# A kernel of two transformer blocks on one Trainium2 core: the values of two groups of attention heads stand together behind every second unit of projection

## The reference, cut to what matters

```python
for qs in range(0, s, Q_BLOCK):                      # forgetting attention, two blocks of 128 queries
    qe = qs + Q_BLOCK
    logits = (jnp.einsum('bhqd,bhkd->bhqk', q[:, :, qs:qe], k[:, :, :qe])
              + cum[:, :, qs:qe, None] - cum[:, :, None, :qe])
    p = jax.nn.softmax(jnp.where(causal, logits, -jnp.inf), axis=-1)
    outs.append(jnp.einsum('bhqk,bhkd->bhqd', p, v[:, :, :qe]))
...
m = jnp.max(scores, axis=-1, keepdims=True)          # window attention
p = jnp.exp(scores - m)
s = jnp.sum(p, axis=-1, keepdims=True)
out = jnp.einsum('bdnqhk,bdnkhe->bdnqhe', p, vc) / s.transpose(0, 1, 2, 4, 3, 5)
```

## Time and profile before

| | |
|---|---|
| median of three runs | 705.66 us (705.50 to 706.17) |
| the profiled execution | 705.47 us, of it 703.7 us in the span |
| PE, matmuls | 687.7 us busy, 98% |
| PE, weight loads (beside the matmuls) | 558.5 us, 79% |
| DVE | 496.7 us, 71% |
| ACT | 381.0 us, 54% |
| DMA | 138.75 MB, mean 197 GB/s |
| chain that ended last, by engine | PE 83%, DVE 7%, ACT 4%, issue 2%, SPq 2%, DMA 2% |

### The profile page before, as it was taken

The page is one execution under the profiler, slowest core; times in us unless marked ns, Lnnn a source line. Parts: engine busy times, 40 slices in busy tenths (PEclk is TensorE's granted clock), DMA queues, the critical chain, the costliest instruction groups (busy, mean ns, idle before and its releaser), DMA issues.

```text
span 703.7 us, 10828 instructions
## 1 busy us (share of the span) xinstructions
PE 687.7 (98%) x4267; PEld 558.5 (79%) x4267; DVE 496.7 (71%) x726; ACT 381.0 (54%) x559; POOL 16.4 (2%) x34
## 2 busy tenths in 40 slices
PE   8899999999999999999999999999999999999996
PEld 4679997777878887877778877778888888888885
DVE  4888988787976779765577889766666555555445
ACT  5457434565655665654565765745474445444344
POOL 6000000000000000000000000000000000000000
PEclk9999999999999999999999999999999999999999
DMA  9999865666896276832444554432656655655511
GB/s 295 367 381 365 287 224 174 204 218 236 302 329 210 57 240 217 280 115 93 145 149 150 183 178 121 150 120 91 196 179 195 207 176 175 190 184 197 187 60 60
DMA packets 74401, 138.75 MB, mean 197 GB/s; under 512 B 5732, under 2 KB 18400, under 8 KB 74352
## 3 DMA queue, kind: packets, MB, share of 16 engines
q1 hardware_dynamic: 72816, 134.92, 58.3%
q10 hardware_dynamic: 736, 1.81, 0.7%
q0 software_dynamic: 800, 1.35, 0.6%
HBM read 137.01 MB, written 1.05 MB: 196 GB/s over the span
## 4 chain that ended last, share of the span: by engine, by line
PE 83%; DVE 7%; ACT 4%; issue 2%; SPq 2%; DMA 2%; DVEq 0%; ACTq 0%
PE G L392 23%; PE G L394 22%; PE G L393 22%; PE T L433 4%; DVE wlo L1108 2%; DMA raw<-in_ret_w_in_dram 2%; PE T L804 1%; PE G L412 1%; PE T L792 1%; PE G L414 1%; PE G L413 1%; DVE arena L1117 1%; SPq L2489 1%; ACT whi L1892 1%; DVE acc L1117 1%
## 5 line engine op out<-in xcount | busy, mean ns | idle before, releaser
L1108 DVE TENSOR_TENSOR wlo<-raw,whi 128x1024 fp32r<-128x1024 f32 x202 | 246.1, 1222 | 119.5 <-ACT whi L1892 119.0
L1892 ACT ACTIVATE whi<-raw 128x1024 fp32r<-128x1024 f32 x202 | 212.6, 1061 | 136.4 <-PE G L394 91.3
L392 PE MATMUL G<-whi,ahi 128*128 128x512 f32 x696 | 281.4, 404 | 0.7 <-DVE wlo L1108 0.7
L394 PE MATMUL G<-whi,alo 128*128 128x512 f32 x696 | 271.8, 390 | 0.0
L393 PE MATMUL G<-wlo,ahi 128*128 128x512 f32 x696 | 271.2, 390 | 0.0
L392 PEld LDWEIGHTS G<-whi,ahi 128*128 128x128 f32 x696 | 130.7, 188 | 30.1 <-DVE wlo L1108 3.0
L394 PEld LDWEIGHTS G<-whi,alo 128*128 128x128 f32 x696 | 130.6, 188 | 28.5
L393 PEld LDWEIGHTS G<-wlo,ahi 128*128 128x128 f32 x696 | 130.9, 188 | 25.5 <-issue 1.0
L1894 ACT ACTIVATE arena<-T,st 128x128 f32<-128x128 f32 (+2 forms) x56 | 21.7, 478 | 33.3 <-DVE st L1502 33.3
L412 PE MATMUL G<-ahi,whi 128*128 128x256 f32 x128 | 36.4, 285 | 0.9 <-DVE wlo L1108 0.9
L1892 ACT ACTIVATE ahi<-T 128x512 fp32r<-128x512 f32 x25 | 15.0, 599 | 40.6 <-PE T L433 40.6
(11 more groups left out here) (245 smaller groups left out, 623.8 us busy)
## 6 DMA issues: line engine op xcount, KB each, us to landing
raw<-in_ret_w_in_dram SPq DMA_DIRECT2D x48, 512.0 KB, 5.4
raw<-in_w_gate_up_dram SPq DMA_DIRECT2D x40, 512.0 KB, 3.6
raw<-in_mod_w_dram SPq DMA_DIRECT2D x32, 512.0 KB, 4.9
raw<-in_fox_w_in_dram SPq DMA_DIRECT2D x32, 512.0 KB, 4.8
raw<-in_w_in_dram SPq DMA_DIRECT2D x28, 512.0 KB, 3.6
raw<-in_w_down_dram SPq DMA_DIRECT2D x22, 512.0 KB, 3.2
arena<-in_mod_w_dram SPq DMA_DIRECT2D x16, 512.0 KB, 10.4
raw<-in_ret_w_out_dram SPq DMA_DIRECT2D x16, 512.0 KB, 5.5
```

The costliest lines, as they stand in the source:

```text
L392: e.matmul(o, ah, wh, start=first and k == 0, stop=False)
L394: done = e.matmul(o, al, wh, start=False, stop=last and k == 1)
L1108: e.tensor_tensor(o, a, b, op).then_inc(sig[name], 1)
L1892: d = e.activation(o, a, f, scale=scale)
```

## The change

`attention_steps` puts the values of groups i - 3 and i - 2 into every second step, i odd, where each step had those of one group. `values` takes bank 0 for an odd group, and bank 3 for an even one.

```diff
 def attention_steps(n):
 
-    return [[("flip", i - 1)] * (1 <= i <= n) + [("logits", i + z) for z in range(2)] * (i < n and i % 2 == 0) + [("values", i - 2)] * (i >= 2)
-            for i in range(n + 2)]
+    return [[("flip", i - 1)] * (1 <= i <= n) + [("logits", i + z) for z in range(2)] * (i < n and i % 2 == 0)
+            + [("values", i - 3 + z) for z in range(2)] * (i >= 3 and i % 2 == 1) for i in range(n + 2)]
...
-                t = bank((name, "values", g), sig[f"{name}_out"], 2 * g + 2, 3)
+                t = bank((name, "values", g), sig[f"{name}_out"], 2 * g + 2, 0 if g % 2 else 3)
```

## The result

The changed kernel took 709.2 us (median of five runs, 707.6 to 709.7), the kernel before 705.7 us (705.5 to 706.67). The ratio is 1.0046, with a 95% interval from 1.0035 to 1.0057: slower by 0.46%. The profiled execution of the changed kernel took 709.7 us, 707.2 of it in the span, 3.5 us more than before.

What follows compares the result with a forecast made beforehand. PE, busy 98% of the span, was taken to bound the kernel. Plain terms of +2.46 us and +1.54 for the clock, on the profiled 705.47, gave 709.5; the median stands 0.19 above, so 709.7 us, range 707.3 to 710.8.

Steps and rivals of the forecast that it cites:

- steps 2 to 8, three pairs: Forgetting attention, groups 0 to 5: each pair of value blocks saves 0.11 us on PE, together -0.33 us.
- step 10, wait for group 7: Forgetting attention: PE's first mask waits for the second `weighted` of DVE, let go at 345.68 instead of 344.93, +0.75 us.
- step 11, unit to `left_of`: Forgetting attention: `left_of` needs group 9's `weighted` and stalls PE 2.84 us; 2.2 or 3.9 also possible.
- the clock: Behind the step 11 stall PE's granted clock falls to 0.50, costing +1.54 us; chance 0.50 as part of the forecast.
- steps 12 and 13: Forgetting attention's end: values 10 move to stand ahead of values 11, saving 0.23 us.
- window attention: Two pairs give -0.22 us and steps 6 and 7 -0.23, together -0.45 us, with no new wait.
- A pair against two blocks: On PE a values block costs 0.61 us before other work, 0.50 before another block: 0.11 us saved per pair.
- Step 6 and the other even steps: Forgetting attention: the mask's new wait for the odd group's `weighted` is over before the mask is due; nothing waits.
- The copy at step 9: DVE's copy of flip 8, ending at 344.31, hangs on ACT and DVE, so it stays where it was.
- the stall alone: Rival: all waits as forecast, but the granted clock stays at its higher level, 708.1 us; chance 0.28.
- Not slower: Rival: DVE comes through step 11 in time, `left_of` never waits; 704.7 us, or 703.7; chance 0.10.
- The waits breed more: Rival: stall of 3.9 us, or late transposes hold up ACT and next units; 710.8 us or more; chance 0.12.

Runs made afterwards that it cites:

- the bank alone: Kernel before with its steps as they were, only the odd groups' values in bank 0 instead of 3: 709.4 us, and 709.61 us once more.
- the repeat: The changed kernel once more, unaltered, beside the kernel before: 708.21 us, ratio 1.004.
- the stall filled: Changed kernel with 24 unused transposes on PE between values 9 and `left_of` at step 11: 707.5 us, ratio 1.0022.

## Why the prediction was right, point by point

Distances on PE in the profiled executions, before and after:

| stretch | forecast | measured | from |
|---|---|---|---|
| steps 2 to 8, three pairs | -0.33 | -0.34 | flip to logits of step 8: 305.96 to 335.63, and 306.02 to 335.35 |
| step 10, wait for group 7 | +0.75 | +0.74 | 1.21 for 0.47 |
| step 10, values 8 gone | -0.61 | -0.60 | mask to unit: 1.57 for 2.17 |
| step 11, unit to `left_of` | +3.33 | +3.48 | 7.53 for 4.05 |
| the clock | +1.54 | +1.46 | 4.71 for 3.25, `left_of` to flip |
| steps 12 and 13 | -0.23 | -0.48 | flip to unit: 2.04 for 2.52 |
| window attention | -0.45 | -0.62 | 29.60 for 30.22 |
| sum | +4.00 | +3.64 | span: +3.5 |

- **What bounds the kernel.** That PE has next to no slack behind the attention held. The distances add up to 3.64 us and the span grew by 3.5. Step 0 was 0.06 us later from the start, and 0.20 us came back between the attentions, at one set of transposes above all: before, they started at 362.77, 0.51 us behind the matmul ahead of them, right after DVE's product into `acc` (361.43 + 1.29 = 362.72); in the changed kernel they follow after 0.23 us. The list of waits doesn't show that wait.
- **A pair against two blocks.** Right to a few hundredths: the second block costs 1.09 - 0.61 = 0.48 us, 0.50 had been reckoned. The rule on a drain at a change of tiling mode (the Trainium skill, TensorEngine Tiling (Array Packing), Key Properties) would have allowed a larger gain. What the traces show is that logits to unit takes as long as logits to values (346.96 - 345.39 = 1.57 us from mask to unit now, 346.49 - 344.93 = 1.56 from mask to values in the earlier trace rows), so leaving out the values there saved the block and no transition on top.
- **Step 6 and the other even steps.** Right: no wait for group 3, 1 or 5, nor in the window attention.
- **The copy at step 9.** The prediction says that it hangs on ACT and DVE and not on PE, "so it is where it was". Had that held, PE would have waited for it until the same moment, and the -0.33 us of the first three pairs would have been lost there, though the sum counts them. The trace shows that the copy moved with PE: it starts at 343.35 instead of 343.63, by 0.28 us, and so do ACT's exponentials of step 8 (337.19 for 337.47) and PE's logits from which they come (335.35 for 335.63). So the sum was right here against its own reasoning.
- **Step 10.** Right in size. The reads of a pair are further apart on DVE than I had taken: the second reciprocal starts 0.11 us after the multiplication before it ended (344.16 + 0.42 to 344.69), where 0.04 had been taken over from reciprocal to multiplication. The wait made up for it by a shorter latency.
- **Step 11.** Right in mechanism, and 0.15 us too small: the same 0.07 us, twice on the way (the pair at step 9, the pair at step 11). That DVE would not catch up the 0.7 us was right: from the copy of flip 8 to the first reciprocal of step 11 it is 9.91 us now (343.35 to 353.26), and 9.17 before (343.63 to 352.80), 0.74 more.
- **Steps 12 and 13.** The sign was right, the size half of what came. The missing term is a wait that the change takes away. In the kernel before, the values of groups 10 and 11 both stand in bank 3 with only `left_of` between them, so those of group 11 had to wait until DVE had read group 10:

```profile
355.87 0.29 DVE L1108 TENSOR_TENSOR acc<-T,st 128x128 f32<-128x128 f32 x1
...
356.30 0.69 PE L804 MATMUL T<-arena 128*64 128x65 f32 x16
```

  The read ends at 355.87 + 0.29 = 356.16 and the values start 0.14 us later, the usual distance from DVE to PE here. The copy of the flip, for which they wait too, had ended at 355.72. From `left_of` to values 11 it took 0.76 us (355.54 to 356.30); in both traces of the bank alone, where group 11 has bank 0, the same sequence takes 0.59 us (359.86 to 360.45 and 359.34 to 359.93), and in the changed kernel, where `left_of` stands behind transposes instead of values, 0.53 (359.63 to 360.16). The difference, 0.76 - 0.53 = 0.23 us, is what the forecast lacked, within 0.02. In the window attention a unit stands between the last two groups, and there each of the first two pairs gave 0.15 us instead of 0.11 (460.32 to 466.96 before, 464.45 to 470.94 after) and the last steps 0.31 instead of 0.23; what these 0.04 to 0.08 us are isn't resolved.
- **The clock.** The price was right: 1.54 us forecast, 1.46 measured, and 1.58 and 1.54 in the two traces of the bank alone (4.83 and 4.79 for 3.25). That it falls was given 0.50 against 0.28 for the stall alone, and both happened, in different executions of one kernel: seven runs to four. The forecast of 709.7 us was that of an execution with the fall, the rival of 708.1 that of one without it (707.3 to 707.7). The median of 709.2 lies near the first because four of these five runs had the fall, which is in part luck: in the repeat it was three of six, and the median 708.21. That the profiled execution took just 709.7 us is luck too, for its span grew by 3.5 us and not by 4.0, and 2.5 us lay around it instead of 1.8. The Trainium skill, TensorE: Matmul & The Clock Gate, Part 1, says that an idle TensorE goes down to 1.2 GHz and that the point at which the clock changes varies from run to run. The traces agree with both: behind stalls of 3.0, 2.2 and 2.2 us the lower level began at 354.20, 354.05 and 354.79 us, before the end of the stall, 0.2 us and 1.4 us after it.
- **The other rivals.** "Not slower" fell with the 2.96 us of waiting. "The waits breed more" fell too: PE's list of waits has no new row for the time behind the stall, neither in the trace with the slow stretch nor in the one without.

## What to carry to other kernels

When work moves to another buffer, list who takes that buffer next and look in the trace for when its reader finishes: the buffer's next user inherits the wait, and here that user was a step that had nothing to do with the values. Where a wait is for a slow engine, look at what that engine does first at that place and whether it is idle just before; reading the values ahead of a weight tile that had not arrived cost nothing and took away the wait of 0.6 us at step 10. And where TensorE bounds the kernel, count a stall on it as more than its length: one of 2 to 3 us cost 1.5 us again in most executions, 13 of 21 by their spans.

## What the runs showed of the hardware

- The same program at the same stall lost the clock in one profiled execution (3.4 us at 0.50) and kept it in another, so one trace doesn't settle whether a stall costs its length or half as much again. Times of the changed kernel spread over 2.1 us and more, those with the stall filled over 0.5.
- The lower clock near 21 us, from which the price was taken, comes and goes as well: of the two traces of the bank alone, the same program, the first has it (23.0 to 26.4 us) and the second does not. There it costs the whole nothing that can be seen. Of the twelve traces seven have it, and the first mask of step 0 starts at 297.04 to 297.59 us in them, and at 297.09 to 297.51 us in the five without it. So a fall has a price behind step 11, where PE works without a gap, and none that shows near the start, where PE waits for DVE three more times after it (0.62, 0.41 and 0.38 us at L529); that such waits take it up is likely, but was not tried. Nor can it be what parts the two heaps of times: the fast trace of the change has it.
- Two dependent small DVE operations stand 0.04 us apart from reciprocal to multiplication, and 0.11 us from multiplication to the next reciprocal. Why the two differ was not tried.
